# FF1 of a decoder block with its weight pieces as the stationary operand and a transposed output

## The reference

```python
x = x + jnp.einsum("bsd,de->bse", mixed, w_out[l])
h = _rmsnorm(x, ln2_w[l])
u = jax.nn.relu(jnp.einsum("bsd,df->bsf", h, w_ff1[l]))
x = x + jnp.einsum("bsf,fd->bsd", jnp.square(u), w_ff2[l])
```

## Time and profile before

| what | us |
|---|---|
| device time, median of 3 runs | 1605.41 (1605.33 to 1605.66) |
| span of the profiled execution, first to last instruction | 1603.7 |
| TensorE busy | 1583.6 (99%) |
| VectorE busy | 914.4 (57%) |
| ScalarE busy | 745.5 (46%) |

### The profile page before, as it was taken

One profiled execution on the slowest core, in us unless ns is written; L12 is line 12 of the kernel. 1 busy time (PEld: TensorE's weight loads), 2 busy tenths in 40 slices (PEclk: granted clock), 3 DMA queues, 4 the chain that ended last, 5 costly groups with the idle time before them and its releaser, 6 DMA issues.

```text
span 1603.7 us, 20006 instructions
## 1 busy us (share of the span) xinstructions
PE 1583.6 (99%) x7552; PEld 1321.9 (82%) x7552; DVE 914.4 (57%) x1040; ACT 745.5 (46%) x827; POOL 56.9 (4%) x61
## 2 busy tenths in 40 slices
PE   7999999999999999999999999999999999999999
PEld 5888888888878888887888888888888888888887
DVE  5766534777774755646755555554444455554443
ACT  5555434676643443434444544443343444443342
POOL 1000000000041202020000000000000000000000
PEclk9999989999999999999999999999999999999999
DMA  7555543444433333334475555555555555555552
GB/s 252 181 208 184 188 154 129 160 158 151 164 131 132 131 109 126 131 105 165 151 264 186 191 182 190 185 191 184 187 205 184 188 192 180 191 185 203 202 200 82
DMA packets 140518, 275.92 MB, mean 172 GB/s; under 512 B 7088, under 2 KB 7600, under 8 KB 140208
## 3 DMA queue, kind: packets, MB, share of 16 engines
q1 hardware_dynamic: 136160, 272.71, 50.7%
q10 hardware_dynamic: 4304, 2.47, 0.5%
HBM read 273.06 MB, written 2.10 MB: 172 GB/s over the span
## 4 chain that ended last, share of the span: by engine, by line
PE 96%; DVE 2%; ACT 1%; DMA 1%; issue 1%; ACTq 0%; SPq 0%; DVEq 0%
PE acc L354 85%; PE wk L370 2%; PE wk L551 1%; PE wk L572 1%; PE wk L569 1%; PE wk L485 1%; DMA raw<-in_w_in 1%; PE wk L448 1%; PE wk L475 1%; PE wk L435 0%; ACT hi L700 0%; DVE lo L1068 0%; DVE st_lo L1106 0%; PE wk L459 0%; PE wk L539 0%
## 5 line engine op out<-in xcount | busy, mean ns | idle before, releaser
L1068 DVE TENSOR_TENSOR lo<-raw,hi 128x1024 fp32r<-128x1024 f32 x512 | 630.2, 1235 | 585.9 <-ACT hi L700 568.4
L700 ACT ACTIVATE hi<-raw 128x1024 fp32r<-128x1024 f32 x512 | 540.5, 1059 | 609.0 <-PE acc L354 606.9
L354 PE MATMUL acc<-hi,st_hi 128*128 128x512 f32 x1312 | 527.8, 402 | 4.8 <-DVE lo L1068 2.9
L354 PE MATMUL acc<-lo,st_hi 128*128 128x512 f32 x1312 | 513.7, 392 | 0.0
L354 PE MATMUL acc<-hi,st_lo 128*128 128x512 f32 x1312 | 512.4, 391 | 0.0
L354 PEld LDWEIGHTS acc<-hi,st_hi 128*128 128x128 f32 x1312 | 247.7, 189 | 55.5 <-issue 4.3
L354 PEld LDWEIGHTS acc<-lo,st_hi 128*128 128x128 f32 x1312 | 247.2, 188 | 53.0
L354 PEld LDWEIGHTS acc<-hi,st_lo 128*128 128x128 f32 x1312 | 247.8, 189 | 49.5 <-issue 1.9
L354 PE MATMUL acc<-hi,u_hi 128*128 128x512 f32 x512 | 199.3, 389 | 0.0
L354 PE MATMUL acc<-lo,u_hi 128*128 128x512 f32 x512 | 199.2, 389 | 0.0
L354 PE MATMUL acc<-hi,u_lo 128*128 128x512 f32 x512 | 199.2, 389 | 0.0
(11 more groups left out here) (235 smaller groups left out, 1123.3 us busy)
## 6 DMA issues: line engine op xcount, KB each, us to landing
raw<-in_w_ff SPq DMA_DIRECT2D x128, 1024.0 KB, 5.2
raw<-in_w_in SPq DMA_DIRECT2D x100, 1024.0 KB, 4.9
raw<-in_w_out SPq DMA_DIRECT2D x16, 1024.0 KB, 5.1
raw<-in_w_gdn_proj SPq DMA_DIRECT2D x8, 1024.0 KB, 5.0
raw<-in_w_swa_proj SPq DMA_DIRECT2D x4, 1024.0 KB, 4.9
x_tok<-in_x SPq DMA_DIRECT2D x2, 1024.0 KB, 7.3
x<-in_x SPq DMA_DIRECT2D x1, 2048.0 KB, 7.7
out_x<-x ACTq DMA_DIRECT2D x3, 512.0 KB, 3.5
```

The lines of the kernel that those rows point to most:

```text
L354: last = pe.matmul(acc[:, t], w[:, k0 + 2 * m + kk, P * t:P * t + P], v[:, i % PIECES, kk, :], start=m == 0 and kk == 0 and a == 0, stop=m ...
L700: act.activation(hi[:, i % PIECES], raw[:, i // 2 % RAW, 2 * (i % 2):2 * (i % 2) + 2, :], ACT.Copy)\
L1068: dve.tensor_tensor(lo[:, i % PIECES], raw[:, i // 2 % RAW, 2 * (i % 2):2 * (i % 2) + 2, :], hi[:, i % PIECES].bitcast(F32), ALU.subtract) ...
```

## The change

FF1 gets a PE function of its own, `group_t`. The weights are now stationary (128 columns of a piece) and the activations move (256 tokens), so that the output has the hidden features on the partitions, which is the layout that `u_hi` and `u_lo` need. Bank t holds features 256t to 256t+255 of the 512, and a place has 12 matmuls of 256 columns in the place of 6 of 512. The transposes `u_turn` are gone, and `uq` is read straight from SBUF. The factor `rstd2` now goes along the columns: DVE makes `r_diag` (the identity times the factor, for both halves of the tokens), PE multiplies it with ones (`spread_r`), which gives the factors as a row on every partition, and DVE copies that to `r_rows`. DVE then reads the banks, ReLU and factor in one instruction (`scaled_relu`), which ACT did before. The whole of the added and removed code is here but for the places in memory and the names of the events.

```diff
+            def group_t(q, g, n, mid={}, after={}):
+                place = 0
+                for pair in range(n // 2):
+                    for t in range(TT):
+                        for m in (2 * pair, 2 * pair + 1):
+                            if t == 0:
+                                pe.wait_ge(lo_ready, 8 * q + m + 1)
+                            if m == 0:
+                                pe.wait_ge(acc_free, 2 * g + 1 + t)
+                            for kk in range(2):
+                                for c in range(2):
+                                    at = P * (2 * t + c)
+                                    for a, (v, w) in enumerate(((hi, st_hi), (hi, st_lo), (lo, st_hi))):
+                                        last = pe.matmul(acc[:, t, TT * P * c:TT * P * c + TT * P],
+                                                         v[:, m % PIECES, kk, at:at + P], w[:, 2 * m + kk, :],
...
-            def u_turn(half, g, first=False):
-                def step():
-                    pe.wait_ge(ev["u_squared"], g + 8 * half + 1)
...
-                    turn(lambda t, b: uq[:, t, P * b:P * b + P], tbv, ev["u_turned"])
-                return step
...
+            def spread_r():
+                pe.wait_ge(ev["r_diag"], 2)
+                pe.matmul(wk[:, 2, 0:TT * P], ones[:], r_diag[:].rearrange("p t n -> p (t n)"), start=True, stop=True)\
+                    .then_inc(ev["r_sum"], 1)
+
             for half, (qf, qg, gf, gg_) in enumerate(((QF0, QG0, GF0, GG0), (QF1, QG1, GF1, GG1))):
-                group(qf, gf, 8, st_hi, st_lo, after={} if half else {1: x_turn(3), 5: wait_e})
-                group(qf + 1, gf + 1, 8, st_hi, st_lo, after={1: u_turn(half, 0, True)})
-                with pe.Fori(2, 8) as g:
-                    group(qf + g, gf + g, 8, st_hi, st_lo, after={1: u_turn(half, g - 1)})
+                group_t(qf, gf, 8, after={} if half else {1: x_turn(3), 4: spread_r, 5: wait_e})
+                with pe.Fori(1, 8) as g:
+                    group_t(qf + g, gf + g, 8)
...
-                group(qg, gg_, 16, u_hi, u_lo, after={1: u_turn(half, 7), 13: wait_u})
+                group(qg, gg_, 16, u_hi, u_lo, after={13: wait_u})
...
-                    f(u_hi[:, span(4 * g, 4), :], tbv, ACT.Copy, None, ev["u_hi"])
+                    f(u_hi[:, span(4 * g, 4), :], uqv, ACT.Copy, None, ev["u_hi"])
...
+            def r_diagonal():
+                dve.wait_ge(ev["e_square"], 4)
+                for t in range(TT):
+                    ts_(r_diag[:, t, :], ident[:], rstd2[:, t:t + 1], None, ALU.mult, None, None, ev["r_diag"])
+
+            def r_copy():
+                dve.wait_ge(ev["r_sum"], 1)
+                dve.tensor_copy(r_rows[:], wk[:, 2, 0:TT * P]).then_inc(ev["r_rows"], 1)
+                dve.wait_ge(ev["r_rows"], 1)
+
+            def scaled_relu(q, g):
+                def half_of(t):
+                    dve.scalar_tensor_tensor(out=us[:, t].rearrange("p (b t) -> p b t", t=TT * P),
+                                             in0=acc[:, t].rearrange("p (b t) -> p b t", t=TT * P), scalar=0.0,
+                                             in1=bcast(r_rows[:], 1, [P, 2, TT * P]), op0=ALU.max, op1=ALU.mult)\
+                        .then_inc(acc_free, 1)
...
+                ahead(qf, 8, {} if half else {1: x_lo(3), 4: r_diagonal, 6: r_copy}, read_out=scaled_relu(qf, gf))
+                u_square(gf)
+                with dve.Fori(1, 8) as g:
+                    ahead(qf + g, 8, {2: u_lo_step(half, g - 1)}, read_out=scaled_relu(qf + g, gf + g))
+                    u_square(gf + g)
```

More of the change, by code:

```diff
@@ L80 @@
     n_wT n_S n_o0 n_Sc n_ws n_qs n_vn1 n_qe n_o1 n_oc n_sq n_nss n_nl n_nr n_on n_out d_turned d_hi d_lo
-    m_mixed x_back e_turned e_hi e_lo e_square u_squared u_turned u_hi u_lo stored c_gate angles ab_act
+    m_mixed x_back e_turned e_hi e_lo e_square u_squared u_hi u_lo r_diag r_sum r_rows stored c_gate angles ab_act
     ab_vec g_vec n_init""".split()
@@ L356, in group @@
                                                      stop=m == n - 1 and kk == 1 and a == 2)
+                            if t == 1:
+                                last.then_inc(piece_used, 1)
+                            elif m == n - 1:
+                                last.then_inc(acc0_done, 1)
+                            steps = after if place % 2 else mid
+                            if place // 2 in steps:
+                                steps[place // 2]()
+                            place += 1
+            def group_t(q, g, n, mid={}, after={}):
[13 more added lines that the diff above has]
+                                                         v[:, m % PIECES, kk, at:at + P], w[:, 2 * m + kk, :],
+                                                         start=m == 0 and kk == 0 and c == 0 and a == 0,
+                                                         stop=m == n - 1 and kk == 1 and c == 1 and a == 2)
                             if t == 1:
@@ L1027, in step @@
                 def step():
-                    wait_apart(ev["u_turned"], g + 8 * half + 1)
-                    f(u_hi[:, span(4 * g, 4), :], tbv, ACT.Copy, None, ev["u_hi"])
-                return step
[L1032 to L1035, removed]
+                    wait_apart(ev["u_squared"], g + 8 * half + 1)
+                    f(u_hi[:, span(4 * g, 4), :], uqv, ACT.Copy, None, ev["u_hi"])
+                return step
             for half, (qf, qg, gf, gg_) in enumerate(((QF0, QG0, GF0, GG0), (QF1, QG1, GF1, GG1))):
[L1038 to L1044, removed]
+                ahead(qf, 8, {} if half else {1: x_hi(3), 3: x_stats})
+                with act.Fori(1, 8) as g:
+                    ahead(qf + g, 8, {2: u_hi_step(half, g - 1)})
                 ahead(qg, 16, {2: u_hi_step(half, 7)})
@@ new lines, in r_copy, with first, second @@
+            def r_copy():
[8 more added lines that the diff above has]
+                        .then_inc(acc_free, 1)
+                def first():
+                    dve.wait_ge(acc0_done, g + 1)
+                    half_of(0)
+                def second():
+                    dve.wait_ge(piece_used, 8 * q + 8 + PIECES)
+                    half_of(1)
+                return first, second
```

23 lines of the change are left out of this document (5 added, 18 removed).

## The result

| kernel | median, us | runs |
|---|---|---|
| before | 1605.37 (1604.20 to 1605.66) | 4 |
| changed | 1618.69 (1617.73 to 1618.73) | 4 |

The ratio is 1.0081, with a 95% interval from 1.0067 to 1.0095: the change makes the kernel slower by 13.3 us. The forecast was 1600.8 us; the result is the second rival, for which 1618 us stood there.

The account below looks back on a forecast made before the run. TensorE bounds the kernel, busy 1583.6 of 1603.7 us. FF1 gain -11.3 us (14.6 less 3.3), stall +5.1 and clock +1.6 give -4.6 us: 1605.4 to 1600.8 us, 0.3% faster; range 1594 to 1610.

Parts of the forecast that it names:

- the second rival: FF1 matmuls: the excess is paid by each matmul, 120.0 ns at 256 columns; +12.6 us, 1618 us; chance 0.14.
- Removed: the transposes: FF1 on PE: 128 transposes, 8 in each of 16 groups, are all on the path and worth 14.6 us.
- Changed: the width: FF1: 96 matmuls of 512 columns a group become 192 of 256 at 114.4 ns; 3.3 of the 14.6 us paid back.
- The upper bound of the step: FF1 pitch at 256 columns: if all 13.3 ns over 2.4 GHz are paid once for each matmul, 120.0 ns.
- The comparison with plain float32: Plain float32 at 128 columns, 110 ns a matmul, taken to show load and stream near their limits without adding up.
- The stall: First FF1 group: PE waits for `r_diag` at `spread_r` behind place 9, so place 10 starts 5.1 us late.
- The clock: After PE's idle near 907: fall to 1.2 GHz for at least 3.2 us of work; 1.6 us lost, at most about 3.
- The read-out: Moved from ACT to DVE: two instructions a group of 0.76 us each, without PE waiting for the banks.
- the break-even of 115.9 ns: FF1 pitch at which the changed kernel is no faster: 22.25 us a group.

Follow-up runs that it names:

- experiment 2: Kernel before, transposes kept, each FF1 matmul of 512 columns made as two of 256; 1625.09 us, ratio 1.0121.
- 5: Kernel before, FF1 matmuls moving only the first 384 (first half) or 320 (second half) of 512 columns; 1512.09 us, work left out.
- 6: Kernel before, FF1 matmuls moving only the first 448 (first half) or 288 (second half) of 512 columns; 1524.83 us, work left out.
- 3: Changed kernel with the spreading matmul behind place 13, only 64 of 128 weight columns loaded in FF1; 1600.41 us, features left out.
- 7: Changed kernel with late spreading matmul, 96 (first half of FF1) or 112 (second) of 128 weight columns loaded; 1602.01 us, features left out.
- Experiment 1: Changed kernel with the spreading matmul moved from behind place 9 to behind place 13 of the first FF1 group; 1610.82 us, ratio 1.0034.
- 10: Changed kernel with late spreading matmul, 32 (first half of FF1) or 80 (second) weight columns loaded; 1598.82 us, work left out.
- 4: Changed kernel with late spreading matmul, consecutive FF1 matmuls writing to different PSUM banks in turn; 1610.33 us, half of the hidden features left out.
- 11: Kernel before, FF1 products reordered so that two matmuls in a row load the same stationary block; 1604.15 us.
- 9: Kernel before at 512 columns, 64 (first half of FF1) or 32 (second) of 128 token columns loaded; 1609.54 us, work left out.
- 12: Changed kernel with late spreading matmul, both FF1 operands read as bfloat16 (upper 16 bits); 1590.16 us.
- 14: Kernel before at 512 columns, FF1 in bfloat16 for all three products (first half) or only the cross terms (second); 1608.01 us.

## Why the prediction was wrong

- **Removed: the transposes, 14.6 us.** Right: experiment 2 kept them, and the account closes with them within the spread of the runs.
- **Changed: the width.** This is the step that failed. It took 114.4 ns for 256 columns because "the difference is 217 ns for 496 columns, 0.4375 a column: most of the excess is paid by the column". Measured were 120.0 ns, 17.2 us more over 3072 matmuls than the step had, which is nearly all of the 17.9 us between forecast and result. The two durations were real, but a duration is not a pitch, and one was of a matmul that streams 16 columns behind a wide one. What experiments 2, 5 and 6 showed in its place: with a full load of 128 columns, some 12 to 16 ns are paid for each matmul from 256 to 512 columns wide. The upper bound of the step, made from the 226.7 ns and no second row, was the value itself.
- **The comparison with plain float32** was a wrong guide too: a plain float32 record of 256 columns takes 215 ns, under 2 over the 213.3 of half the speed, and says nothing of a float32r one that streams twice as fast; experiments 3 and 7 show that at 256 float32r columns the load does matter.
- **The stall, 5.1 us.** Right in place and cause: `r_diag` was foretold for 907.1 and came at 907.6, PE idled 4.03 us, and place 10 began 4.9 us late. **The clock, 1.6 us.** The mechanism was right and the size was off: the low clock held for 5.5 us of FF1's matmuls and not 3.2, and cost 2.6 us, within the 3 us named as the upper bound. Together that is 7.5 us by the trace against 6.7. Experiment 1 puts it at 7.9 us and leaves the 0.4 us of the spreading matmul, which the 5.1 include, in the kernel.
- **The read-out.** Right: 688 ns an instruction against the 760 taken, no wait of PE.
- **The rivals.** "The excess is paid by the matmul" had its pitch of 120.0 ns and its price right, +12.6 us against 13.3 measured, and got a chance of 0.14 only. As a rule it holds for the full load that this change has; experiments 3, 7 and 10 show the excess to change with the load. The pitch lies over the break-even of 115.9 ns, so the kernel is slower.

The Trainium skill (TensorE: Matmul & The Clock Gate, Back-to-back issue gap) says that in a stream of pairs load and matmul both set the spacing. Experiments 3, 7 and 10 agree with that in kind, with 113.3 to 120.0 ns at one width for different loads, though not in one direction; its fixed part of 2.5 ns at full clock is not what any float32r row here shows.

**What stays open** is why the excess is what it is. It is not the bank (4), the block that is loaded (11), which operand is stationary (2), a share of the moved columns (5, 6) or of the loaded ones (9, 10), nor float32r alone (12, 14). At half clock it vanishes: 256 columns at 1.2 GHz are 213.3 ns, and the twenty matmuls from 909.13 us on in the changed kernel start 213.5 ns apart. That streams with a load of 64 and of 32 have two stable pitches each speaks for load and stream falling into step with each other; this is argued, not shown. In experiments 5, 6, 9 and 14 plain float32 transposes stand in each group, and whether their pitches would be others without these was not tried (at 512 columns with the full load FF2, which has none behind its first group, shows the same 226.7 ns); nor were contiguous bfloat16 operands.

## What to carry to other kernels

Take the price of a matmul from starts, over many in a row, and treat what is over columns / 2.4 GHz as paid by the instruction until a second width shows otherwise: halving the width of a stream that already fills TensorE cost 6.7 ns of every 113.3 here, more than the transposes it saved. Before one puts a wait into the one full engine, one should look at what stands ahead of the releasing instruction in its own engine's order; moving the wait by four places was worth 7.9 us. An experiment that changed the width and nothing else settled what the rows could not.

## What the runs showed of the hardware that was not expected

- At 256 float32r columns moved, 113.3 ns or 120.0 with 64 columns loaded, 113.3 with 80, 116.0 with 96, 117.8 with 112, 120.0 with 128, but 117.8 or 120.0 with 32.
- At 512 columns, shorter loads make the matmul slower: 226.7, 230.0 and 231.5 ns with 128, 64 and 32 loaded, with transposes in each group.
- One plain float32 matmul in a stream with a load of 64 moves all that follow from 113.3 to 120.0 ns, and a wide float32r matmul behind it undoes this; with a load of 32 it moves them from 120.0 to 117.7 ns, and with 96 or 128 it changes nothing.
- Float32r and bfloat16 matmuls mixed in one stream are slower than either type alone at 512 columns: 234.1 against 226.7 and 225.0 ns.
